# Token tiles and the first two weight units loaded and used in halves, constants and memory tokens loaded later

## The chip, the cores and the metric

The kernel runs on one core of one Trainium2 chip. Times are microseconds (us) of device time of one execution. The engines are TensorE (PE: matmuls and transposes, with PEld its weight loads), VectorE (DVE), ScalarE (ACT), GpSimd (POOL) and SyncE (SP), which issues nearly all transfers.

## What is computed

One inference step of a decoder layer, for a prompt of 256 tokens and 8 sample tokens together, so 264 columns of activations, with D_MODEL = 1024 and D_FF = 2816. Cut to its parts:

```python
x = x + 0.5 * swiglu_ffn(x, ffn1_norm, ffn1_w_in, ffn1_w_out)      # gate, up = split(rmsnorm(x) @ w_in); (silu(gate) * up) @ w_out
h = rmsnorm(x, mix_norm); proj = h @ w_in                          # pooling input, q, k, v, memory query
y = concat(pool_mixer, block-sparse attention over paged K/V, attention over 256 memory tokens)
x = x + y @ w_out
x = x + 0.5 * swiglu_ffn(x, ffn2_norm, ffn2_w_in, ffn2_w_out)
```

The memory keys and values of the prompt are computed here as well: `rmsnorm(mem_prompt) @ mem_w_kv`, and the keys are normed by head. The new keys, values and pooling state are outputs too.

## The kernel before

The kernel is one program written out by hand for each engine; semaphores order the engines, and each engine runs its own list in order. Activations lie transposed in SBUF: `xT` has 8 tiles of 128 channels by 264 tokens. Every matmul of a weight is done in three passes (`three`, L1381): a high part times a high part, high times low, low times high. So each weight unit of 128 x 1024 values goes through four steps: SP loads it into one of four `raw` buffers (`load_unit`, L414, issue on L421), ACT rounds it to `w_hi` (`split`, L632, L638), DVE subtracts to get `w_lo` (`split`, L910, L914), and PE runs 24 matmuls with it (L1383 to L1385), then raises `w_used`. The ring has RING = 4 slots: `load_unit` waits until DVE is through with the unit four before (`lo_ready`), and ACT's `split` waits until PE is through with it (`w_used`).

The first feed-forward has 44 such units, numbered 0 to 43 here; two of them (gate and up) give one of 22 hidden tiles. For each hidden tile DVE scales the gate (`gate`, L950), ACT does the Silu (L663), DVE scales the up half, multiplies, rounds and subtracts (`up_hidden`, L955 to L964). DVE's list for a pair of units is: split, gate, split, the four steps of up_hidden. ACT's list is: split, Silu, split. PE must wait for `gu_free`, raised by L955, before it writes over a pair of PSUM banks. Iterations 2 to 5 run in a loop on every engine, 6 to 10 stand singly because work on the memory tokens lies between them (`M_TURN_AT = 6`: PE transposes `m_rows` into four banks, ACT makes `m_hi` on L773, DVE `m_lo` on L1177). Four units of `mem_w_kv` follow, then 22 units of `ffn_w_out`.

The start, in program order. POOL sets constants. ACT loads `ident` and `gains` by its own queue. SP issues the sample tokens, the two prompt tiles (128 x 1024 each), units 0 to 3, `m_rows` (the memory tokens, 1 MB), the page table, nine constants, four pieces of `pool_w` and a copy of the pooling state; then it goes on with unit 4 and, from unit `EARLY_KEYS` = 7 on, pages of the key cache between the units. PE runs AWAKE = 20 matmuls on ones (each is two instructions in the profile, L1564), then 24 transposes of `x_rows` into 8 banks (L1391): the four lower tiles of sample and first prompt tile, then the four of the second prompt tile, then the upper four tiles. ACT copies the odd tiles out (L742) and rounds all eight to `x_hi` (L744, L746), two tiles per step of its loop, with `split(0)` and `split(1)` after the first two steps. DVE copies the even tiles (L1133), makes `x_lo` (L1138) and `w_lo`. PE then takes units 0 and 1 interleaved by channel tile. Behind that ACT squares the token rows (L754, with a root on L756, three times), DVE makes diagonals of the reciprocals and PE turns them into a row of scales (L1597). ACT goes on with split(4), split(5), the squares of the memory tokens (L762) and their root (L764), the load of the Silu table (L666), split(6).

## Time and profile before

| what | value |
|---|---|
| median of 3 runs | 602.05 us (600.65, 602.05, 602.41) |
| profiled execution, whole | 600.45 us |
| its span in the profile | 598.7 us |
| mean granted clock of PE | 0.991 |
| PE busy | 571.6 us, 95% of the span |
| DVE busy | 395.1 us, 66% |
| ACT busy | 263.5 us, 44% |
| DMA | 128.41 MB, mean 214 GB/s |

The profiled execution has 1.75 us around its span. It is 1.60 us below the median of the runs shown. A row of the timeline gives the start, the duration, the engine, the line, what is written and read, and in brackets the idle time before it with what ended it. Consecutive instructions of a line are merged into one row with their count.

### The profile page before, as it was taken

The page shows a single profiled execution, that of the slowest core. Times are in us where ns is not written, and L with a number is a line of the kernel's source. Part 1 is how long each engine was busy: PE and PEld are TensorE (multiplying, and loading weights), DVE is VectorE, ACT ScalarE, POOL GpSimd, SP SyncE. Part 2 cuts the span into 40 slices and gives each one's busy share as a digit, 9 for nine tenths or more (in the row PEclk, how much of TensorE's full clock was granted, in tenths as well). Part 3 has the DMA queues.
Part 4 walks back from the last instruction along what each step waited for, and adds up shares of the span by engine and source line. Part 5 has one row for each costly group of instructions (what it writes and reads, how often), then busy time and mean ns, then how long its engine had stood idle before and what let it go on. Part 6 is the DMA issues. An engine that isn't in the chain of part 4 may idle for free.

```text
span 598.7 us, 13514 instructions
## 1 busy us (share of the span) xinstructions
PE 571.6 (95%) x5124; PEld 524.9 (88%) x5124; DVE 395.1 (66%) x713; ACT 263.5 (44%) x410; POOL 16.1 (3%) x24
## 2 busy tenths in 40 slices
PE   7999999999999999999899758999999999999997
PEld 6999999999899997666567536989999999999996
DVE  3577677777598878699766530468767676774443
ACT  4843434534543337254376531474343434353331
POOL 1000000000000003000000000030000000000000
PEclk9899999999999999999999998999999999999999
DMA  9968778775677544997974799347665566575522
GB/s 284 293 177 249 224 227 239 223 235 177 211 233 276 193 142 139 327 386 219 372 261 140 237 358 362 96 117 211 175 176 174 171 178 174 180 236 185 175 71 73
DMA packets 132801, 128.41 MB, mean 214 GB/s; under 512 B 6560, under 2 KB 103927, under 8 KB 132751
## 3 DMA queue, kind: packets, MB, share of 16 engines
q1 hardware_dynamic: 132471, 127.76, 66.7%
q8 instruction: 26, 0.43, 0.3%
q10 hardware_dynamic: 288, 0.08, 0.1%
q14 instruction: 16, 0.13, 0.1%
HBM read 125.12 MB, written 2.83 MB: 214 GB/s over the span
## 4 chain that ended last, share of the span: by engine, by line
PE 69%; DVE 14%; issue 5%; ACT 4%; SPq 4%; DMA 3%; DVEq 0%; ACTq 0%; POOL 0%; POOLq 0%
PE banks L1383 21%; PE banks L1384 20%; PE banks L1385 20%; DVE w_lo L914 4%; DVE kv L925 3%; SPq L456 3%; ACT w_hi L638 2%; DMA kv<-in_cache_v 2%; PE banks L1522 2%; PE banks L1391 1%; SPq L442 1%; PE banks L1564 1%; PE banks L1798 1%; DMA raw<-in_ffn_w_in 1%; PE banks L1492 1%
## 5 line engine op out<-in xcount | busy, mean ns | idle before, releaser
L914 DVE TENSOR_TENSOR w_lo<-raw,w_hi 128x1024 fp32r<-128x1024 f32 x160 | 195.7, 1230 | 109.4 <-ACT w_hi L638 108.9
L1383 PE MATMUL banks<-x_hi,w_hi 128*128 128x264 f32 x768 | 222.1, 289 | 5.8 <-DVE w_lo L914 3.0
L1384 PE MATMUL banks<-x_lo,w_hi 128*128 128x264 f32 x768 | 218.4, 284 | 0.0
L1385 PE MATMUL banks<-x_hi,w_lo 128*128 128x264 f32 x768 | 218.2, 284 | 0.0
L638 ACT ACTIVATE w_hi<-raw 128x1024 fp32r<-128x1024 f32 x160 | 164.1, 1052 | 81.7 <-PE banks L1385 66.2
L1383 PEld LDWEIGHTS banks<-x_hi,w_hi 128*128 128x128 f32 x768 | 145.3, 189 | 10.4 <-issue 4.2
L1384 PEld LDWEIGHTS banks<-x_lo,w_hi 128*128 128x128 f32 x768 | 145.5, 189 | 0.0
L1385 PEld LDWEIGHTS banks<-x_hi,w_lo 128*128 128x128 f32 x768 | 144.8, 189 | 0.0
L1383 PE MATMUL banks<-h_hi,w_hi 128*128 (+1 forms) x352 | 100.3, 285 | 0.0
L1385 PE MATMUL banks<-h_hi,w_lo 128*128 (+1 forms) x352 | 100.2, 285 | 0.0
L1384 PE MATMUL banks<-h_lo,w_hi 128*128 (+1 forms) x352 | 100.0, 284 | 0.0
L663 ACT ACTIVATE sg<-sg 128x264 f32<-128x264 f32 x44 | 18.7, 426 | 142.1 <-DVE sg L950 142.1
L1384 PEld LDWEIGHTS banks<-h_lo,w_hi 128*128 128x128 f32 x352 | 66.5, 189 | 0.0
L1383 PEld LDWEIGHTS banks<-h_hi,w_hi 128*128 128x128 f32 x352 | 66.2, 188 | 0.3 <-ACT mem_kv L784 0.3
L1385 PEld LDWEIGHTS banks<-h_hi,w_lo 128*128 128x128 f32 x352 | 66.3, 188 | 0.0
L925 DVE STREAM_TRANSPOSE kv<-kv 128x1024 f32<-128x1024 f32 x32 | 38.6, 1228 | 0.0
L1383 PE MATMUL banks<-w_hi,x_hi 128*128 128x512 f32 x64 | 27.9, 435 | 0.8 <-DVE w_lo L914 0.7
L1385 PE MATMUL banks<-w_hi,x_lo 128*128 128x512 f32 x64 | 25.3, 395 | 0.0
L1384 PE MATMUL banks<-w_lo,x_hi 128*128 128x512 f32 x64 | 25.3, 395 | 0.0
L964 DVE TENSOR_TENSOR h_lo<-h_tmp,h_hi 128x264 f32 (+1 forms) x44 | 19.1, 434 | 3.6
L960 DVE TENSOR_TENSOR h_tmp<-sg,h_tmp 128x264 f32<-128x264 f32 x44 | 19.1, 433 | 2.6 <-ACT sg L663 1.3
L1798 PEld LDWEIGHTS banks<-kv,p_cols 128*8 128x8 f32 x512 | 13.4, 90 | 7.2 <-issue 7.2
(269 smaller groups left out, 498.2 us busy)
## 6 DMA issues: line engine op xcount, KB each, us to landing
raw<-in_ffn_w_in SPq DMA_DIRECT2D x88, 512.0 KB, 4.5
raw<-in_ffn_w_out SPq DMA_DIRECT2D x44, 512.0 KB, 3.4
kv<-in_cache_k SPq DMA_DIRECT2D x64, 256.0 KB, 5.1
kv<-in_cache_v SPq DMA_DIRECT2D x64, 256.0 KB, 4.8
raw<-in_w_in SPq DMA_DIRECT2D x12, 512.0 KB, 3.8
raw<-in_w_out SPq DMA_DIRECT2D x8, 512.0 KB, 6.0
raw<-in_mem_w_kv SPq DMA_DIRECT2D x4, 512.0 KB, 3.5
raw<-in_w_in SPq DMA_DIRECT2D x8, 256.0 KB, 3.7
```

Source lines behind the costliest of these rows:

```text
L456: sp.dma_start(kv[t % 4::4, slot, t // 4 * 2048:(t // 4 + 1) * 2048].rearrange("k (b c) -> k b c", b=4), cache[0, ds(page, 1)].rearrange(" ...
L638: act.activation(w_hi[:, n % RING, :], raw[:, n % RING, :], ACT.Copy).then_inc(hi_ready, 1)
L663: act.activation(sg[:, s, :], sg[:, s, :], ACT.Silu).then_inc(silu_ready, 1)
L914: vec.tensor_tensor(w_lo[:, n % RING, :], raw[:, n % RING, :], w_hi[:, n % RING, :].bitcast(F32), ALU.subtract).then_inc(lo_ready, 1)
L925: vec.transpose(key_pair(g), key_pair(g)).then_inc(k_turned8, 1)
L960: vec.tensor_tensor(h_tmp[:, s, :], sg[:, s, :], h_tmp[:, s, :], ALU.mult).then_inc(hm_ready, 1)
L964: vec.tensor_tensor(h_lo[:, ds(c, 1), :].rearrange("p a n -> p (a n)"), h_tmp[:, s, :], h_hi[:, ds(c, 1), :].rearrange("p a n -> p (a n)") ...
L1383: pe.matmul(out, lhs[0], rhs[0], start=start, stop=False)
L1384: pe.matmul(out, lhs[0], rhs[1], start=False, stop=False)
L1385: return pe.matmul(out, lhs[1], rhs[0], start=False, stop=stop)
L1522: mm = pe.matmul(bank[LG_BANK][32 * hp:32 * hp + 32, half * NP:(half + 1) * NP], q_cols[:, c0:c0 + 32], keys[:, 4 * hp + c], start=(b4 == ...
L1798: mm = pe.matmul(out, p_cols[:, 2 * half + t // 4, r0:r0 + 8], kv[:, slot, c0:c0 + P], start=False, stop=(b4 == 3 and t == PAGES - 1))
```

## The change

AWAKE goes from 20 to 10 and EARLY_KEYS from 7 to 8. The prompt tiles are loaded as four transfers of 128 x 512 instead of two of 128 x 1024; units 0 and 1 are loaded as two transfers of 4 x 128 columns each. ACT, DVE and PE use them by halves: PE transposes tiles 0 to 3 completely and then 4 to 7, ACT rounds half a unit after each of its four steps, DVE subtracts half a unit at a time, and PE runs unit 0 and then unit 1 over channel tiles 0 to 3, then both over 4 to 7. The page table, the constants, `m_rows`, `pool_w` and `band` are issued by SP at the ends of iterations 1 to 5 of the first feed-forward. ACT's squares of the memory tokens stand at the ends of iterations 4 and 5, their root behind the last Silu, with the Sqrt table loaded there instead of behind `mem_kv`; DVE's reciprocal of that root stands after the feed-forward.

```diff
--- before.py
+++ after.py
@@ -55,7 +55,7 @@
 TURN_BANKS = {5: 6, 0: 6, 1: 0, 2: 6, 3: 1, 4: 7}
 HY_BANKS, POOL_BANKS, MK_BANKS, QM_BANK = (6, 7, 4), (4, 5), (6, 4), 7
 ACT_PAGES = (0, 2, 4, 6)
-EARLY_PAIRS, AWAKE = 16, 20
+EARLY_PAIRS, AWAKE = 16, 10
 UNITS = 12
 X_BANKS = (4, 5, 6, 7, 0, 1, 2, 3)
 M_FIRST = (2, 3, 0, 1, 4, 5, 6, 7)
@@ -64,7 +64,7 @@
 J_ORDER = (2, 3, 0, 1)
 M_EARLY = (5, 6, 7, 0, 1, 3, 4)
 SQ_AFTER = (1, 3, 5)
-EARLY_KEYS, LATE_KEYS = 7, 9
+EARLY_KEYS, LATE_KEYS = 8, 9
 KV_SLOTS = 4
 KEPT = ("k", 0), ("k", 1), ("k", 6), ("k", 7)
 HELD = (4, 5, 6, 7)
@@ -247,6 +247,7 @@
         pg_loaded, poolw_loaded = sem("pg_loaded"), sem("poolw_loaded")
         raw_loaded = [sem(f"raw_loaded{i}") for i in range(RING)]
         kv_loaded = [[sem(f"kv_loaded{i}_{h}") for h in range(2)] for i in range(KV_SLOTS)]
+        first_loaded, first_hi, first_lo = [sem("first_loaded0"), sem("first_loaded1")], sem("first_hi"), sem("first_lo")
         hi_ready, lo_ready, w_used = sem("hi_ready"), sem("lo_ready"), sem("w_used")
         const_set = sem("const_set")
         lead_ready = sem("lead_ready")
@@ -477,25 +478,42 @@
                     sp.dma_start(kv[:, slot, :].rearrange("p (b t c) -> p b t c", b=NS, t=2),
                                  cache[0].rearrange("b (t p) h d -> p b t (h d)", p=P)).then_inc(kv_loaded[slot][0], 16)
 
+            def load_first(j, half):
+                col = j % 2 * DFF
+                sp.dma_start(raw[:, j, half * 512:(half + 1) * 512].rearrange("p (k c) -> p k c", k=4),
+                             ffn_in[0][:, 4 * half:4 * half + 4, col:col + P]).then_inc(raw_loaded[j] if half else first_loaded[j], 16)
+
             sp.dma_start(x_rows[0:NS, 0, :], a["x_sample"][:, 0, :]).then_inc(x_loaded[0], 16)
-            for t in range(2):
-                sp.dma_start(x_rows[:, 1 + t, :], a["x_prompt"][0, t * P:(t + 1) * P, :]).then_inc(x_loaded[t], 16)
-            for j in range(4):
+            for half in range(2):
+                for t in range(2):
+                    cols = slice(half * 512, half * 512 + 512)
+                    sp.dma_start(x_rows[:, 1 + t, cols], a["x_prompt"][0, t * P:(t + 1) * P, cols]).then_inc(x_loaded[half], 16)
+                load_first(half, 0)
+            for j in range(2):
+                load_first(j, 1)
+            for j in range(2, 4):
                 load_unit(U_FFN1, j, 0, ffn_in[0][:, :, (j // 2) * P + (j % 2) * DFF:(j // 2) * P + (j % 2) * DFF + P])
-            sp.dma_start(m_rows[:], a["mem_prompt"][0].rearrange("(t p) d -> p t d", p=P)).then_inc(m_loaded, 16)
-            sp.dma_start(page_ids[:], a["page_table"].rearrange("b g -> (b g)").unsqueeze(0)).then_inc(pg_loaded, 16)
-            for j, name in enumerate(("k_norm", "mem_k_norm", "q_norm")):
-                sp.dma_start(head_gain[:, j, :], a[name][0].partition_broadcast(P)).then_inc(c_loaded, 16)
-            for dst, name in ((rope, "rope"), (samp, "samp"), (rank, "rank"),
-                              (causal, "causal"), (band, "band")):
-                sp.dma_start(dst[:], a[name]).then_inc(c_loaded, 16)
-            sp.dma_start(ext[NS:P, :], a["state_pool"][0].rearrange("b j c -> (b j) c")).then_inc(c_loaded, 16)
-            sp.wait_ge(const_set, 2)
-            for g in range(4):
-                lo = HD * (g % 2)
-                sp.dma_start(pool_wd[lo:lo + HD, g // 2, lo:lo + HD], a["pool_w"][0, g]).then_inc(poolw_loaded, 16)
-            sp.dma_start(a["state_out"][0, :, 0:BUF - 1, :], a["state_pool"][0, :, 1:BUF, :]).then_inc(stored, 16)
-            sp.wait_ge(pg_loaded, 16)
+            def load_constants(i):
+
+                if i == 1:
+                    sp.dma_start(page_ids[:], a["page_table"].rearrange("b g -> (b g)").unsqueeze(0)).then_inc(pg_loaded, 16)
+                    for j, name in enumerate(("k_norm", "mem_k_norm", "q_norm")):
+                        sp.dma_start(head_gain[:, j, :], a[name][0].partition_broadcast(P)).then_inc(c_loaded, 16)
+                    sp.wait_ge(pg_loaded, 16)
+                elif i == 2:
+                    for dst, name in ((rope, "rope"), (samp, "samp"), (rank, "rank"), (causal, "causal")):
+                        sp.dma_start(dst[:], a[name]).then_inc(c_loaded, 16)
+                    sp.dma_start(ext[NS:P, :], a["state_pool"][0].rearrange("b j c -> (b j) c")).then_inc(c_loaded, 16)
+                elif i == 3:
+                    sp.dma_start(m_rows[:], a["mem_prompt"][0].rearrange("(t p) d -> p t d", p=P)).then_inc(m_loaded, 16)
+                elif i == 4:
+                    sp.wait_ge(const_set, 2)
+                    for g in range(4):
+                        lo = HD * (g % 2)
+                        sp.dma_start(pool_wd[lo:lo + HD, g // 2, lo:lo + HD], a["pool_w"][0, g]).then_inc(poolw_loaded, 16)
+                    sp.dma_start(a["state_out"][0, :, 0:BUF - 1, :], a["state_pool"][0, :, 1:BUF, :]).then_inc(stored, 16)
+                elif i == 5:
+                    sp.dma_start(band[:], a["band"]).then_inc(c_loaded, 16)
 
             pages_at = {EARLY_KEYS + p * 3 // 2: p for p in range(3 * PAGES)}
             for i in range(1, HT // 2):
@@ -504,6 +522,7 @@
                     load_unit(U_FFN1, j, i, ffn_in[0][:, :, col:col + P])
                     if 4 * i + j in pages_at:
                         load_page(*divmod(pages_at[4 * i + j], PAGES))
+                load_constants(i)
             for j in range(4):
                 load_unit(U_MEM, j, 0, w_mem[:, 2 * j:2 * j + 2, :])
             for k in range(HT):
@@ -744,8 +763,10 @@
                 act.activation(x_hi[:, odd - 1, :], xT[:, odd - 1, :], ACT.Copy, scale=gains[:, odd - 1:odd]).then_inc(xhi_ready, 1)
                 act.wait_ge(xT_act, pair + 1)
                 act.activation(x_hi[:, odd, :], xT[:, odd, :], ACT.Copy, scale=gains[:, odd:odd + 1]).then_inc(xhi_ready, 1)
-                if pair < 2:
-                    split(pair)
+                n, half = pair % 2, pair // 2
+                cols = slice(half * 512, half * 512 + 512)
+                act.wait_ge(raw_loaded[n] if half else first_loaded[n], 16)
+                act.activation(w_hi[:, n, cols], raw[:, n, cols], ACT.Copy).then_inc(hi_ready if half else first_hi, 1)
             split(2)
             split(3)
             junk = tmp[:].rearrange("p k n -> p (k n)")[:, 0:D]
@@ -757,22 +778,24 @@
                     .then_inc(xroot_ready, 1)
             split(4)
             split(5)
-            act.wait_ge(m_loaded, 16)
-            for t in range(2):
-                act.activation(m_junk[:, t, :], m_rows[:, t, :], ACT.Square, accum_out=ms[:, t:t + 1]).then_inc(ms_ready, 1)
-            act.wait_ge(ms_ready, 2)
-            act.activation(m_root[:], ms[:], ACT.Sqrt, bias=eps_col[:, 0:1], scale=1.0 / D).then_inc(mroot_ready, 1)
             table(ACT.Silu, 0)
             split(6)
             silu(0, 0, 0)
             ffn_second(0)
-            ffn_in_loop(0, 2, M_TURN_AT)
+            ffn_in_loop(0, 2, M_TURN_AT - 1)
+            act.wait_ge(m_loaded, 16)
+            act.activation(m_junk[:, 0, :], m_rows[:, 0, :], ACT.Square, accum_out=ms[:, 0:1]).then_inc(ms_ready, 1)
+            ffn_in_loop(0, M_TURN_AT - 1, M_TURN_AT)
+            act.activation(m_junk[:, 1, :], m_rows[:, 1, :], ACT.Square, accum_out=ms[:, 1:2]).then_inc(ms_ready, 1)
+            act.wait_ge(ms_ready, 2)
             for part in range(4):
                 for k in (2 * part, 2 * part + 1):
                     act.wait_ge(m_turned, k // 2 + 1)
                     act.activation(m_hi[:, k, :], bank[k // 2][:, (k % 2) * NP:(k % 2 + 1) * NP], ACT.Copy,
                                    scale=gains[:, 16 + k:17 + k]).then_inc(mhi_ready, 1)
                 ffn_in_loop(0, M_TURN_AT + part, M_TURN_AT + part + 1 if part < 3 else HT // 2)
+            table(ACT.Sqrt, 1)
+            act.activation(m_root[:], ms[:], ACT.Sqrt, bias=eps_col[:, 0:1], scale=1.0 / D).then_inc(mroot_ready, 1)
             for j in range(2, 6):
                 split(U_MEM + j)
             act.wait_ge(mrstd_ready, 1)
@@ -782,7 +805,6 @@
                 else:
                     act.wait_ge(w_used, U_MEM + 4)
                 act.activation(mem_kv[:, t, :], bank[t][:, :], ACT.Copy, scale=m_rstd[:, t:t + 1]).then_inc(mkv_ready, 1)
-            table(ACT.Sqrt, 1)
             ffn_out_loop(0, 0, 1)
             act.wait_ge(mkv_ready, 2)
             head_squares(0, ALL, mem_kv[:, :, 0:256])
@@ -1138,16 +1160,24 @@
                     vec.scalar_tensor_tensor(out=x_lo[:, m, :], in0=xT[:, m, :], scalar=gains[:, m:m + 1],
                                              in1=x_hi[:, m, :].bitcast(F32), op0=ALU.mult, op1=ALU.subtract).then_inc(xlo_ready, 1)
 
+            def split_half(n, half):
+                cols = slice(half * 512, half * 512 + 512)
+                vec.wait_ge(hi_ready if half else first_hi, n + 1)
+                vec.tensor_tensor(w_lo[:, n, cols], raw[:, n, cols], w_hi[:, n, cols].bitcast(F32), ALU.subtract)\
+                    .then_inc(lo_ready if half else first_lo, 1)
+
             x_copy(0)
             x_copy(2)
             x_lo_pair(0)
-            split(0)
+            split_half(0, 0)
+            x_lo_pair(1)
+            split_half(1, 0)
             x_copy(4)
-            x_lo_pair(1)
-            split(1)
             x_copy(6)
             x_lo_pair(2)
+            split_half(0, 1)
             x_lo_pair(3)
+            split_half(1, 1)
             split(2)
             split(3)
             vec.wait_ge(id_loaded, 16)
@@ -1166,8 +1196,6 @@
             gate(0, 0, 0, U_FFN1)
             up_hidden(0, 0, 0, U_FFN1)
             ffn_second(0)
-            vec.wait_ge(mroot_ready, 1)
-            vec.reciprocal(m_rstd[:], m_root[:]).then_inc(mrstd_ready, 1)
             ffn_in_loop(0, 2, M_TURN_AT)
             vec.wait_ge(ms_ready, 2)
             for part in range(4):
@@ -1178,6 +1206,8 @@
                                              scalar=gains[:, 16 + k:17 + k], in1=m_hi[:, k, :].bitcast(F32),
                                              op0=ALU.mult, op1=ALU.subtract).then_inc(mlo_ready, 1)
                 ffn_in_loop(0, M_TURN_AT + part, M_TURN_AT + part + 1 if part < 3 else HT // 2)
+            vec.wait_ge(mroot_ready, 1)
+            vec.reciprocal(m_rstd[:], m_root[:]).then_inc(mrstd_ready, 1)
             for j in range(2, 6):
                 split(U_MEM + j)
             vec.wait_ge(c_loaded, 16 * 9)
@@ -1563,28 +1593,24 @@
             for _ in range(AWAKE):
                 pe.matmul(bank[X_BANKS[KT - 1]][:, 0:P], ones[:], ones[:], start=True, stop=True)
             pe.wait_ge(id_loaded, 16)
-            pe.wait_ge(x_loaded[0], 32)
-            for m in range(4):
-                turn(bank[X_BANKS[m]][:, 0:NS], x_rows[0:NS, 0, m * P:(m + 1) * P], NS)
-                turn(bank[X_BANKS[m]][:, NS:NS + P], x_rows[:, 1, m * P:(m + 1) * P])
-            pe.wait_ge(x_loaded[1], 16)
-            for m in range(4):
-                turn(bank[X_BANKS[m]][:, NS + P:N], x_rows[:, 2, m * P:(m + 1) * P]).then_inc(x_turned, 1)
-            for m in range(4, KT):
+            pe.wait_ge(x_loaded[0], 48)
+            for m in range(KT):
+                if m == 4:
+                    pe.wait_ge(x_loaded[1], 32)
                 turn(bank[X_BANKS[m]][:, 0:NS], x_rows[0:NS, 0, m * P:(m + 1) * P], NS)
                 turn(bank[X_BANKS[m]][:, NS:NS + P], x_rows[:, 1, m * P:(m + 1) * P])
                 turn(bank[X_BANKS[m]][:, NS + P:N], x_rows[:, 2, m * P:(m + 1) * P]).then_inc(x_turned, 1)
             pe.wait_ge(const_set, 5)
             pe.wait_ge(xT_vec, 1)
             pe.wait_ge(xT_act, 1)
-            for k in range(KT):
-                pe.wait_ge(xlo_ready, k + 1)
+            for half in range(2):
                 for j in range(2):
-                    if k == 0:
-                        pe.wait_ge(lo_ready, j + 1)
-                    mm = three(bank[GU_BANK + j][:, 0:N], weights(j, k * P, (k + 1) * P), (x_hi[:, k, :], x_lo[:, k, :]),
-                               k == 0, k == KT - 1)
-                    if k == KT - 1:
+                    pe.wait_ge(lo_ready if half else first_lo, j + 1)
+                    for k in range(4 * half, 4 * half + 4):
+                        pe.wait_ge(xlo_ready, k + 1)
+                        mm = three(bank[GU_BANK + j][:, 0:N], weights(j, k * P, (k + 1) * P), (x_hi[:, k, :], x_lo[:, k, :]),
+                                   k == 0, k == KT - 1)
+                    if half:
                         mm.then_inc(w_used, 1)
             for j in range(2, 4):
                 pe.wait_ge((xT_vec, xT_act)[j % 2], 2)
```

## Rows read from the trace of the kernel before

**Rows 1.** Timeline of the first 17 us: PE, ACT and SP's queue.
```profile
1.00 3.35 PE L1564 MATMUL banks<-ones 128*128 128x128 f32 x14 [1.00 <-POOL ones L603]
...
7.60 4.25 PE L1391 MATMUL banks<-ident,x_rows 8*128 8x8 f32 x24
...
9.64 0.39 ACT L742 ACTIVATE xT<-banks 128x264 f32<-128x264 f32 x1 [6.39 <-PE banks L1391]
...
14.14 2.49 SPq L496 DMA_DIRECT2D pool_wd<-in_pool_w  x4
```

**Rows 2.** DMA issues at 1.64, 2.11 and 17.55 us: size, issue to landing.
```profile
x_rows<-in_x_prompt SPq DMA_DIRECT2D x1, 512.0 KB, 4.5
...
raw<-in_ffn_w_in SPq DMA_DIRECT2D x1, 512.0 KB, 5.9
...
raw<-in_ffn_w_in SPq DMA_DIRECT2D x1, 512.0 KB, 5.3
```

**Rows 3.** Timeline of ACT, one step of the start and splits 2, 3.
```profile
11.78 0.37 ACT L742 ACTIVATE xT<-banks 128x264 f32<-128x264 f32 x1
...
12.05 0.50 ACT L744 ACTIVATE x_hi<-xT,gains 128x264 fp32r<-128x264 f32 x1
...
12.87 1.05 ACT L638 ACTIVATE w_hi<-raw 128x1024 fp32r<-128x1024 f32 x1
...
16.62 2.00 ACT L638 ACTIVATE w_hi<-raw 128x1024 fp32r<-128x1024 f32 x2
```

**Rows 4.** Timeline of ACT from 22.9 to 29.6 us, splits 4, 5 and 6.
```profile
22.90 1.06 ACT L638 ACTIVATE w_hi<-raw 128x1024 fp32r<-128x1024 f32 x1 [0.18 <-DMA raw<-in_ffn_w_in]
24.68 1.06 ACT L638 ACTIVATE w_hi<-raw 128x1024 fp32r<-128x1024 f32 x1 [0.72 <-DMA raw<-in_ffn_w_in]
25.65 1.04 ACT L762 ACTIVATE m_junk<-m_rows 128x1024 f32<-128x1024 f32 x1
...
28.17 1.28 ACT L666 ACT_TABLE_LOAD   x1
...
29.57 1.04 ACT L638 ACTIVATE w_hi<-raw 128x1024 fp32r<-128x1024 f32 x1
```

**Rows 5.** Timeline of PE: first matmuls of units 2, 4, 8; around unit 16.
```profile
22.56 0.28 PE L1383 MATMUL banks<-x_hi,w_hi 128*128 128x264 f32 x1
...
29.26 0.37 PE L1383 MATMUL banks<-x_hi,w_hi 128*128 128x264 f32 x1
...
40.94 0.28 PE L1383 MATMUL banks<-x_hi,w_hi 128*128 128x264 f32 x1
...
64.11 0.28 PE L1385 MATMUL banks<-x_hi,w_lo 128*128 128x264 f32 x1
64.48 0.38 PE L1383 MATMUL banks<-x_hi,w_hi 128*128 128x264 f32 x1
```

**Rows 6.** Timeline of DVE in the first feed-forward: w_lo of units 8, 16, 20.
```profile
39.08 1.23 DVE L914 TENSOR_TENSOR w_lo<-raw,w_hi 128x1024 fp32r<-128x1024 f32 x1 [1.44 <-ACT w_hi L638]
...
62.78 1.23 DVE L914 TENSOR_TENSOR w_lo<-raw,w_hi 128x1024 fp32r<-128x1024 f32 x1 [1.44 <-ACT w_hi L638]
63.93 0.43 DVE L955 TENSOR_TENSOR h_tmp<-banks,rstd 128x264 f32<-128x264 f32 x1
...
74.86 1.23 DVE L914 TENSOR_TENSOR w_lo<-raw,w_hi 128x1024 fp32r<-128x1024 f32 x1 [1.45 <-ACT w_hi L638]
```

**Rows 7.** Waits from 30 to 150 us: total, times, longest.
```profile
ACT sg L663 <- DVE sg L950: 70.4, 22, 3.8
```

**Rows 8.** Windows: busy time (instructions) of PE, PEld, DVE, ACT, POOL; PEclk, DMA share, GB/s.
```profile
15.33:18.75 3.42, 3.28 (x15) 3.28 (x16) 3.10 (x7) 2.95 (x5) 0.00 (x0) 0.50 0.94 289
```

**Rows 9.** Timeline at the end of the first feed-forward, ACT, DVE and PE.
```profile
150.23 2.00 ACT L638 ACTIVATE w_hi<-raw 128x1024 fp32r<-128x1024 f32 x2
...
152.77 3.49 DVE L914 TENSOR_TENSOR w_lo<-raw,w_hi 128x1024 fp32r<-128x1024 f32 x3
...
155.39 0.39 PE L1383 MATMUL banks<-w_hi,m_hi 128*128 128x512 f32 x1
```

## The prediction, made before the changed kernel ran

> **What bounds the kernel now.** The page says that PE is busy nearly all the time, so I looked for the place where PE's pace comes from, in three steps. First the timeline of the start. PE runs its warm-up matmuls without a pause until the first transpose at 7.60, ACT gets its first tile at 9.64 [rows 1], and then ACT works without a gap until split(3); unit 2 starts on PE at 22.56 [rows 5]. Second, the transfers: the second prompt tile, issued at 1.64, lands 4.5 later, at 6.1, and unit 0, issued at 2.11, lands at 8.0 [rows 1, 2]. The queue passes 512 KB in about 1.9, so units 1, 2, 3 land at 9.9, 11.7, 13.6 (estimate), and behind them stand 1 MB of memory tokens and the constants: unit 4, issued at 17.55 [rows 2], lands at 22.9, where ACT waits for it [rows 4].
>
> Third, the first feed-forward. PE needs 40.94 - 29.26 = 11.68 for four units when nothing holds it [rows 5]. The same four units on DVE, from w_lo of unit 16 to that of unit 20, take 74.86 - 62.78 = 12.08 [rows 6]. ACT waits for DVE before each Silu, 22 times, 70.4 in all [rows 7], and DVE then waits 1.44 for ACT's w_hi [rows 6]: the two pass a baton round, split, up_hidden, split, gate, Silu, split. Neither waits for PE there, since a gate needs a unit that PE finished some 5 us before. And PE stops: after 64.11 it starts the next unit at 64.48, right behind the h_tmp of 63.93 that frees the banks [rows 5, 6]. So from about unit 15 to the end of that feed-forward PE follows the DVE and ACT round. **Its start decides**, the split of unit 6 at 29.57 [rows 4], and not PE's own start alone.
>
> **The change, part by part.**
> *Warm-up.* Twenty matmuls are 40 instructions, 14 of them take 3.35 [rows 1]. Half of them, 20, last from 1.0 to about 5.3 (a step is 0.21 at first, 3.35 less the long first one, over 14). The first halves of the prompt tiles have together as many bytes as one tile now; one tile lands 1.9 before 6.1, so 4.2, and with smaller packets up to 5.0. PE starts to transpose at 5.3 and not at 7.6: 2.2 earlier, with no pause between.
> *Transposes.* 24 take 4.25, three per tile, 0.53 [rows 1]. Tile 0 is ready at 5.9, tile 1 at 6.5, tile 3 at 7.5. The second halves lie behind 256 KB of unit 0: 6.1 + 0.95 + 0.1 = 7.2, in time. Tiles 4 to 7 are ready at 8.0 to 9.6. ACT can start at 6.6 and not at 9.64, because its tile no longer waits for four transposes of the other prompt tile.
> *ACT's four steps.* A copy is 0.27 from start to start, two roundings 0.82, a unit 0.95 [rows 3]. Half a unit I put at 0.58, between a half (0.48) and a whole (0.95), near the half since a rounding of 264 columns is 0.41. A step is 1.67, four are 6.7. One stall comes in: DVE has its copy of tile 4 behind the half splits of units 0 and 1. Half a w_lo I put at 0.6 (half of 1.23), so DVE reaches the copy at 10.8, is done at 11.2 (0.43, as its other operations on 264 columns, [rows 6]), and ACT has waited 0.9. Split(2) starts at 6.6 + 6.7 + 0.9 = 14.3, now 16.62 [rows 3]: 2.3 earlier. By bounds of 0.48 and 0.95 for the half it is 2.7 or 0.8.
> *PE.* It takes unit 0 lower half at 9.6 (behind its last transpose), unit 1 lower at 11.1, unit 0 upper at 13.5, unit 1 upper at 15.2 (w_lo ends then), each 12 matmuls of 0.121 = 1.5. Unit 2 starts at 16.6, when its w_lo is there, and not at 22.56: 5.9 earlier.
> *Units 4 and 5.* Unit 4 is issued when w_lo of unit 0 is whole, at 13.5, with an empty queue: even with the 5.3 of today [rows 2] it lands at 18.8. ACT wants it 2.3 earlier than 22.90 - 0.18, at 20.4. That wait goes, and of the 24.68 of unit 5 another 0.84 (0.72 of it shown as idle). Together 1.0.
> *Squares and root of the memory tokens.* Between split(5), 24.68, and the table load, 28.17, lie 3.49; without them 1.06: 2.4 less [rows 4]. Split(6) comes 2.3 + 1.0 + 2.4 = 5.8 earlier, at 23.8.
> *Where they go.* One square (1.04 [rows 4], and some 0.2 of readout) comes in between the even and the odd split of ACT, at the ends of iterations 4 and 5. DVE takes the odd one only after w_lo (1.15, from 62.78 to 63.93 [rows 6]) and the four steps of up_hidden (some 0.4 each), 2.75 after the even w_hi; ACT has it ready at 0.95. With 1.23 it is 2.2: hidden, with 0.6 to spare. At the second place the m_hi copies come on top, but DVE's m_lo too. Bounds: 0, or 1.2 each.
> *Moved loads.* 14.14 to 16.63 for four `pool_w` [rows 1]: 0.62 each. By this row a small issue costs up to 0.6, so with eleven others and the larger `m_rows` it is about 9 of SP time (estimate), in five pieces of up to some 3. Behind each stands the load of a unit. Such a load is issued when w_lo of the unit four before is there: for unit 20 at 64.0, and its split is at 73.8 (its w_lo begins at 74.86, less 1.05) [rows 6]. That is 9.8, for an odd unit less, about 7.5 (estimate); the load takes up to 5.3 [rows 2], so 2 to 4 are spare. The dearest piece is `m_rows`, 1 MB, 3.8 of the queue before unit 16, which has about 9.8 as unit 20. I take 0, up to 3 in all. Pages one unit later: nothing, they are used in the second matmul stage. SP's wait for the page table holds unit 8 until some 23 to 24, when its own condition (w_lo of unit 4, 22.7) comes as well, and its split is due at 32.
> *Sqrt table.* 1.28 and 0.3 of root are now before the splits of the third and fourth memory unit, at 150.23 [rows 9]. The first of them is then 1.8 late, but DVE took it only at 152.77 [rows 9], so its w_lo comes 0.4 later, at 154.4 in today's times, and PE wants it at 155.39 [rows 9]. Nothing, and DVE's m_rstd hides too. The table behind `mem_kv` goes, beside PE's work: nothing. Without this cover it would be 0.4.
>
> **Sum.** The round of DVE and ACT starts 5.8 earlier, PE is 5.9 earlier at unit 2, and would arrive at unit 8 with today's margin. Everything after is ordered by PE and by buffers that PE frees, the page loads of the attention as well, so the shift goes through to the end. 600.45 - 5.8 = 594.65 for the profiled execution; the median is 1.60 above it, so 596.25 on that base. Between the two, nearer the median, I take **595.9**.
>
> **The clock.** Today PE has two gaps at 13.6 and before, and 15.33 to 18.75 runs at half the granted clock, 0.50, that is 1.2 GHz and not 2.4 [rows 8]. In the changed kernel the gaps are shorter (12.5 to 13.5, a few tenths at 15). If it falls again for one such stretch, PE loses 3.42 x 0.5 = 1.7. But PE loses some 0.4 per four units to the round anyway, so this is covered later: nothing, or at most 0.5 by the row of scales (L1597) for split(6). The Trainium skill ("TensorE: Matmul & The Clock Gate", Part 1: The HAM clock gate) says that the throttled state is the default and that activity releases it, which speaks against halving the warm-up. By that rule the transposes could run at the low clock; the rows agree that gaps cost the clock.
>
> **Rivals.**
> (A) Part of it stays (0.22). ACT's chain is shortened less: half units cost near whole ones (2.7 - 0.8, so 1.5 lost), or both squares show in the round (2.4 lost), or unit 5 is late. Gain 2 to 4.3, around 3.4: 598.7. For: the margin of 0.6 is thin. Against: DVE's order puts 2.75 there.
> (B) Transposes at the half clock (0.08). A matmul at half clock is 0.22 and not 0.12, so four tiles cost 1.7 more, ACT's tile 1 comes 0.5 later and tile 5 about 1.2: gain 4.6, 597.4.
> (C) It does not show (0.06). PE starts earlier, but the attention stage or the page loads are tied to something that does not move, and the gain is waited away: 602. Against: its loads wait for buffers that PE frees.
> (D) Slower (0.06). SP's issues become part of the round: each piece of constants in the feed-forward holds a unit's load beyond its split, and PE stands. Place: units 8 to 24. If all 9 count, it is 602.05 - 5.8 + 9 = 605.3. It decides when more than 2 to 4 per piece is held. Against: ACT waits for a load only twice today, 0.9 in all, both before unit 6.
> (E) Halves cost the queue a fixed part each (0.02). Tile to unit lands 1.9 apart for 512 KB although one transfer takes 4.5 to land: 2.6 is fixed and hidden now. If it fell on each of the four added transfers, unit 3 would land 10.4 later, at 24.0, 8.8 after its split is due: 602.05 - 5.8 + 8.8 = 605.0. The Trainium skill ("DMA: Bandwidth & Descriptors", Rules for kernel authors) advises 1 MiB or more per transfer and to merge small ones, so by it the halves lose; the rows, with transfers that follow each other closely, speak against a loss of this size.
> The forecast itself has 0.56.
>
> **Numbers.** The forecast's own range is 594.0 to 597.3. With (A) and (B) I go to 593.6 and 599.6; above lie (C), (D) and (E), 0.14. A measurement of this kernel can tell about 0.3%, 1.8 us, from no change. Faster by more: forecast, (B) and most of (A), 0.85. Within: 0.08. Slower: 0.07.
>
> **What the profile would show.** First transpose at 5.3 with no gap before; ACT's first tile at 6.6; split(2) at 14.3 with an idle piece of 0.9 before the rounding of tile 4; unit 2 on PE at 16.6; no ACT wait for DMA on units 4 and 5; split(6) at 23.8; w_lo of unit 20 at 69.1; no DVE wait for w_hi above 1.5 at units 23 and 27; the first matmul of the third memory unit at 149.6. The prediction is wrong if ACT waits for `raw` in the feed-forward, if the four-unit step of DVE grows beyond 12.1, or if gaps later on PE grow by what was won.

## The result, and the profile after

The changed kernel takes **594.88 us** (median; 593.37 to 598.02), the kernel before, beside it, 602.23: ratio 0.9888 [0.984, 0.9936], 1.1% faster. A second set of runs of the same kernel, the first experiment below, gave 595.44 against 601.77, ratio 0.9892 [0.9866, 0.9919]. The forecast was 595.9, within 593.6 to 599.6.

The profiled execution of the first set, 598.02 us, is the longest of its set. Its page, in the order busy time, share, instructions; then groups with busy time, mean, idle time before and what ended most of it:

```profile
PE 570.7 (96%) x5104; PEld 523.9 (88%) x5104; DVE 395.5 (66%) x715; ACT 263.1 (44%) x412; POOL 16.1 (3%) x24
...
L936 DVE TENSOR_TENSOR w_lo<-raw,w_hi 128x1024 fp32r<-128x1024 f32 x158 | 193.2, 1230 | 106.6 <-ACT w_hi L657 105.6
```

The page looks like the one before: nearly all that changed lies in the first 30 us. The timeline of that execution answers to [rows 1], [rows 3], [rows 5] and [rows 4]:

```profile
1.00 4.64 PE L1594 MATMUL banks<-ones 128*128 128x128 f32 x20 [1.00 <-POOL ones L622]
...
6.29 6.60 PE L1421 MATMUL banks<-ident,x_rows 8*128 8x8 f32 x24 [0.66 <-DMA x_rows<-in_x_prompt]
...
15.45 1.99 ACT L657 ACTIVATE w_hi<-raw 128x1024 fp32r<-128x1024 f32 x2
...
16.87 0.42 PE L1414 MATMUL banks<-x_lo,w_hi 128*128 128x264 f32 x1
17.09 0.35 PE L1415 MATMUL banks<-x_hi,w_lo 128*128 128x264 f32 x1
17.27 0.29 PE L1413 MATMUL banks<-x_hi,w_hi 128*128 128x264 f32 x1
17.39 0.28 PE L1414 MATMUL banks<-x_lo,w_hi 128*128 128x264 f32 x1
...
24.86 1.04 ACT L657 ACTIVATE w_hi<-raw 128x1024 fp32r<-128x1024 f32 x1
...
27.51 0.43 DVE L1193 COPY rstd<-banks 128x264 f32<-128x264 f32 x1 [2.62 <-PE banks L1623]
...
27.86 1.22 DVE L936 TENSOR_TENSOR w_lo<-raw,w_hi 128x1024 fp32r<-128x1024 f32 x1
```

Two things are to be seen. PE runs at half speed until about 17.1: the 24 transposes take 6.60 where [rows 1] has 4.25, and a matmul step, from one start to the next, is 0.22 up to there and 0.12 from there. And split(6), at 24.86, is not what holds w_lo of unit 6: DVE could have w_hi at 25.90, but stands 2.62 for PE's row of scales (L1623), copies it to `rstd` at 27.51, and starts w_lo(6) only then, at 27.86. w_lo(6) reads nothing of that row. It waits for it because the copy stands ahead of it in DVE's list, and DVE runs its list in order. Below, w_lo(6) is the number to follow. In the kernel before, its two neighbours on DVE were:

```profile
29.54 0.43 DVE L1163 COPY rstd<-banks 128x264 f32<-128x264 f32 x1 [2.53 <-PE banks L1597]
...
30.65 1.23 DVE L914 TENSOR_TENSOR w_lo<-raw,w_hi 128x1024 fp32r<-128x1024 f32 x1 [0.68 <-ACT w_hi L638]
```

There the copy, PE's side, ends at 29.97 (29.54 + 0.43), and ACT's w_hi(6) at 30.61 [rows 4]: **two engines nearly tied**, 0.6 apart.

### The profile page after: what moved, and what is told of

The parts are those of the page before. It is cut to its first block, busy times and chain, and to the rows that moved or that the text cites. A ratio compares the mean times of both kernels' runs of the same rounds, so it can differ in the third digit from the quotient of the medians.

```text
span 596.2 us, 13483 instructions
## 1 busy us (share of the span) xinstructions
PE 570.7 (96%) x5104; PEld 523.9 (88%) x5104; DVE 395.5 (66%) x715; ACT 263.1 (44%) x412; POOL 16.1 (3%) x24
## 4 chain that ended last, share of the span: by engine, by line
PE 75%; DVE 8%; SPq 5%; DMA 4%; issue 4%; ACT 4%; DVEq 0%; ACTq 0%
PE banks L1413 22%; PE banks L1414 22%; PE banks L1415 22%; PE banks L1421 3%; PE banks L1552 2%; DVE w_lo L936 2%; ACT w_hi L657 2%; SPq L457 2%; DMA kv<-in_cache_mem_k 2%; DMA kv<-in_cache_v 1%; SPq L443 1%; DVE kv L947 1%; PE banks L1824 1%; DMA x_rows<-in_x_prompt 1%; PE banks L1522 1%
## 5 line engine op out<-in xcount | busy, mean ns | idle before, releaser
L936 DVE TENSOR_TENSOR w_lo<-raw,w_hi 128x1024 fp32r<-128x1024 f32 x158 | 193.2, 1230 | 106.6 <-ACT w_hi L657 105.6
L657 ACT ACTIVATE w_hi<-raw 128x1024 fp32r<-128x1024 f32 x158 | 161.7, 1050 | 80.2 <-PE banks L1415 71.9
L1824 PE MATMUL banks<-kv,p_cols 128*8 128x128 f32 x512 | 15.9, 280 | 5.2 <-DMA kv<-in_cache_v 5.2
```

Of the source, the lines that this page charges most:

```text
L657: act.activation(w_hi[:, n % RING, :], raw[:, n % RING, :], ACT.Copy).then_inc(hi_ready, 1)
L936: vec.tensor_tensor(w_lo[:, n % RING, :], raw[:, n % RING, :], w_hi[:, n % RING, :].bitcast(F32), ALU.subtract).then_inc(lo_ready, 1)
L1824: mm = pe.matmul(out, p_cols[:, 2 * half + t // 4, r0:r0 + 8], kv[:, slot, c0:c0 + P], start=False, stop=(b4 == 3 and t == PAGES - 1))
```

## The experiments

The theory, R in the texts on record, is the prediction's: the round of DVE and ACT paces the first feed-forward, and its start decides. The text for after_again, written with the first profile at hand, already lets it start at the later of split(6) and the row of scales; the numbers forecast for moved_only still follow split(6) alone. The main rival, P: PE is busy all the time, and its own start decides. Each ran beside the kernel before, which had medians of 601.77, 601.75 and 601.58 in the three sets. Times from the profiles, in us: PE's first matmul of unit 2, ACT's split(6), DVE's w_lo(6), the last matmul of unit 43 (where the first feed-forward's gates end on PE), and the way from w_lo(6) to it.

| kernel | median | unit 2 | split(6) | w_lo(6) | unit 43 | way |
|---|---|---|---|---|---|---|
| before | 601.8 | 22.56 | 29.57 | 30.65 | 149.82 | 119.2 |
| after, first profile | 594.88 | 20.55 | 24.86 | 27.86 | 147.49 | 119.6 |
| after_again | 595.44 | 18.25 | 23.92 | 25.56 | 145.22 | 119.7 |
| awake20 | 595.77 | 18.57 | 25.52 | 26.60 | 146.26 | 119.7 |
| halves_only | 601.76 | 18.94 | 30.63 | 31.70 | 150.66 | 119.0 |
| moved_only | 601.09 | 23.63 | 26.96 | 30.96 | 149.97 | 119.0 |
| scales_early | 595.11 | 19.76 | 24.03 | 25.11 | 144.76 | 119.7 |
| moved_scales | 597.85 | 23.11 | 26.53 | 27.61 | 147.50 | 119.9 |
| pe_delay | 595.47 | 16.88 | 23.83 | 24.91 | 144.56 | 119.7 |
| act_delay | 597.57 | 18.86 | 26.42 | 27.50 | 147.33 | 119.8 |
| x_halves | 599.59 | 22.04 | 25.37 | 29.35 | 148.35 | 119.0 |
| squares_front | 597.38 | 18.93 | 26.42 | 27.50 | 147.13 | 119.6 |
| before_awake10 | 600.35 | 20.74 | 30.69 | 31.77 | 150.82 | 119.1 |
| scales_awake12 | 595.12 | 17.74 | 24.71 | 25.78 | 145.41 | 119.6 |

The median less w_lo(6) is 569.2 to 570.6 in eleven of the fourteen rows, while w_lo(6) itself moves by 6.8: the time follows w_lo(6) nearly one for one. The others are before (571.2), before_awake10 (568.6), and the first profile of after (567.0), which is of the longest execution of its set.

**after_again** is the changed kernel, unedited.

> The changed kernel, untouched, for a second profile. Theory R (the round of DVE and ACT in the first feed-forward sets its end; the round starts at the later of ACT's split(6) and the row of scales, which PE makes behind unit 3): the ratio to before stays near 0.988, and where the granted clock is full during the transposes, unit 2 starts on PE at 16.6 and split(6) at 23.8, w_lo of unit 20 begins at 69.1 and the execution takes 594 to 595. Where the clock is 0.5 until 17 as in the first profile, 598. Rival K (the spread between executions has nothing to do with the clock at the start): the second profile shows the same start whatever its time.

Measured: 595.44, ratio 0.9892 [0.9866, 0.9919]; the profiled execution took 594.74, against 598.02 in the first set, with this start:

```profile
1.00 3.96 PE L1594 MATMUL banks<-ones 128*128 128x128 f32 x20 [1.00 <-POOL ones L622]
5.93 2.13 PE L1421 MATMUL banks<-ident,x_rows 8*128 8x8 f32 x12 [0.98 <-DMA x_rows<-in_x_prompt]
...
7.12 0.39 ACT L761 ACTIVATE xT<-banks 128x264 f32<-128x264 f32 x1 [3.87 <-PE banks L1421]
...
8.89 2.17 PE L1421 MATMUL banks<-ident,x_rows 8*128 8x8 f32 x12 [0.82 <-DMA x_rows<-in_x_prompt]
...
11.55 0.52 ACT L763 ACTIVATE x_hi<-xT,gains 128x264 fp32r<-128x264 f32 x1 [0.82 <-DVE xT L1155]
...
14.51 1.99 ACT L657 ACTIVATE w_hi<-raw 128x1024 fp32r<-128x1024 f32 x2
...
22.52 1.28 ACT L685 ACT_TABLE_LOAD   x1
...
23.92 1.04 ACT L657 ACTIVATE w_hi<-raw 128x1024 fp32r<-128x1024 f32 x1
...
25.21 0.43 DVE L1193 COPY rstd<-banks 128x264 f32<-128x264 f32 x1 [1.26 <-PE banks L1623]
...
25.56 1.22 DVE L936 TENSOR_TENSOR w_lo<-raw,w_hi 128x1024 fp32r<-128x1024 f32 x1
```

The transposes ran at full speed here; the clock was low only for a stretch of PE's first units (windows: busy time and instructions of PE, PEld, DVE, ACT, POOL; PEclk, DMA share, GB/s):

```profile
10.00:14.00 4.00, 4.00 (x22) 3.79 (x22) 3.70 (x9) 3.18 (x9) 0.00 (x0) 0.61 0.96 238
```

It is the same kernel twice, and rival K, the same start in both, is out. With the low clock until 17.1, w_lo(6) is 2.3 later (27.86 for 25.56), and the execution 3.3 longer; the other 1.0 lies behind unit 43, where nothing ties it to the clock of the start. ACT has only 0.94 of the 2.3 (split(6) at 24.86 for 23.92), and by ACT alone w_lo(6) would have been at 25.90. The rest is PE's row of scales.

**awake20** puts the warm-up back to its old length.

```diff
-EARLY_PAIRS, AWAKE = 16, 10
+EARLY_PAIRS, AWAKE = 16, 20
```

> The changed kernel with 20 warm-up matmuls again. Theory R: the transposes cannot start before 7.5, or 9.6 where the clock stays low, ACT is 2.2 later throughout, so half of the gain of the front goes: about 2.2 slower than the changed kernel, some 597.5, ratio 0.992. Rival W (the warm-up buys the clock, and a short one costs more than it frees): as fast as the changed kernel or faster, 593 to 595, ratio 0.988 or below.

Measured: 595.77, ratio 0.9899 [0.9873, 0.9924], 0.3 from after_again. A loss of 2.2 was expected; the medians show none, but the interval just reaches the 0.992 of R. The profile shows half of it:

```profile
26.60 1.23 DVE L936 TENSOR_TENSOR w_lo<-raw,w_hi 128x1024 fp32r<-128x1024 f32 x1 [0.57 <-ACT w_hi L657]
```

On PE the late start of the transposes, 7.52, is paid back by the clock: they run whole and at full speed, 4.25 for 24, and PE reaches unit 2 at 18.57, where after_again, with a stretch at the low clock, is at 18.25. ACT isn't paid back: split(6) is 1.60 later, and w_lo(6) 1.04. Whether the longer warm-up loses that 1.0 these runs can't tell.

**halves_only** keeps the halves and the short warm-up, but has the constants, the memory tokens, the squares and the root where the kernel before has them.

```diff
-            def load_constants(i):
...
+            sp.dma_start(m_rows[:], ...)      # and all constants, ahead of ffn_in_loop
...
+            for t in range(2):
+                act.activation(m_junk[:, t, :], m_rows[:, t, :], ACT.Square, ...)
```

> Halves and the short warm-up, but constants, memory tokens, their squares and root where they were. Theory R: unit 4 lands at 22.9 as before and the squares stand before split(6), so split(6) stays at 29.6 and the time at that of before within 1 us, ratio 1.000. Rival P (PE's own start sets the end): unit 2 starts at 16.6, unit 4 waits for its w_lo until 25.2, and 4 us are won, ratio 0.993.

Measured: 601.76, ratio 1.0001 [0.9984, 1.0018]. **The halves alone bring nothing**, though PE starts unit 2 3.6 earlier:

```profile
23.84 1.06 ACT L649 ACTIVATE w_hi<-raw 128x1024 fp32r<-128x1024 f32 x1 [2.73 <-DMA raw<-in_ffn_w_in]
...
27.98 0.42 DVE L1184 COPY rstd<-banks 128x264 f32<-128x264 f32 x1
...
30.63 1.04 ACT L649 ACTIVATE w_hi<-raw 128x1024 fp32r<-128x1024 f32 x1
31.70 1.23 DVE L927 TENSOR_TENSOR w_lo<-raw,w_hi 128x1024 fp32r<-128x1024 f32 x1 [3.30 <-ACT w_hi L649]
```

ACT waits 2.73 for unit 4, which stands behind the memory tokens in the queue, and its split(6) is at 30.63. PE's side was done at 28.40. R had forecast this result, and P, with 4 us won, is out.

**moved_only** has the constants, squares and root moved, but the tiles and units 0 and 1 whole and the long warm-up.

```diff
-                load_first(half, 0)
+                sp.dma_start(x_rows[:, 1 + t, :], a["x_prompt"][0, t * P:(t + 1) * P, :])...
...
-EARLY_PAIRS, AWAKE = 16, 10
+EARLY_PAIRS, AWAKE = 16, 20
```

> Constants, memory tokens, their squares and root moved, but tiles and units whole and 20 warm-up matmuls. Theory R: split(2) stays at 16.6, the waits for units 4 and 5 (1.0) and the squares (2.4) go, split(6) at 26.1, 3.4 us won, ratio 0.994. Rival P: unit 2 stays at 22.56 on PE and nothing is won, ratio 1.000. Rival D (the loads between the units hold the ring): slower than before.

Measured: 601.09, ratio 0.9982 [0.9965, 0.9999]: a gain of 0.7 where 3.4 was expected. Split(6) did come 2.6 earlier, at 26.96, but:

```profile
26.96 1.04 ACT L646 ACTIVATE w_hi<-raw 128x1024 fp32r<-128x1024 f32 x1
29.54 1.03 PE L1606 MATMUL banks<-x_diag,ones 8*128 8x8 f32 x6
30.61 0.43 DVE L1172 COPY rstd<-banks 128x264 f32<-128x264 f32 x1 [3.62 <-PE banks L1606]
30.96 1.22 DVE L923 TENSOR_TENSOR w_lo<-raw,w_hi 128x1024 fp32r<-128x1024 f32 x1
```

DVE has w_hi(6) at 28.00, but the row of scales, which PE makes behind unit 3 at 29.54, only at 30.61 (the 3.62 of the line count from the end of w_lo(5)). PE was at unit 2 1.07 later than in the profile of before, and the stretch from 14 to 18 us has a granted clock of 0.50 here and 0.67 there, so part of this lateness may be the chance of one execution. Here the sum that follows split(6) alone fell. The theory from here on: w_lo(6) starts at the later of two, w_hi(6) of ACT and the row of scales of PE (R2 in the texts on record). The test is to move one side alone.

**scales_early** is the changed kernel with the row of scales between units 2 and 3.

```diff
+                if j == 2:
+                    for t in range(3):
...
+                    mm.then_inc(xr_psum, 1)
```

> The changed kernel with PE's row of scales between units 2 and 3 instead of behind unit 3. Theory R2 (the round of DVE and ACT starts at w_lo of unit 6, which waits for two things, ACT's split(6) and the row of scales): w_lo of unit 6 begins right behind split(6), 25.0 in place of 25.6 where the clock was up early, 25.9 in place of 27.9 in an execution like the first profile of the changed kernel; 0.5 to 2 us won over the changed kernel, 594, ratio 0.987. Rival P (PE's own start sets the end): no change, or 0.5 slower where PE waits for the diagonals.

Measured: 595.11, ratio 0.988 [0.9848, 0.9912]. The copy moves to 23.97 and w_lo(6) stands right behind ACT:

```profile
23.97 0.42 DVE L1193 COPY rstd<-banks 128x264 f32<-128x264 f32 x1
...
25.11 1.23 DVE L936 TENSOR_TENSOR w_lo<-raw,w_hi 128x1024 fp32r<-128x1024 f32 x1 [0.71 <-ACT w_hi L657]
```

That is 0.45 earlier than in after_again, and nothing that the medians can tell.

**moved_scales** is moved_only with the same edit.

> moved_only (constants, memory tokens and their squares moved; tiles and units whole, 20 warm-up matmuls) with the row of scales between units 2 and 3. Theory R2: moved_only won only 0.7 because its split(6) ended at 28.0 but the row of scales came at 30.9 behind unit 3; now w_lo of unit 6 begins at 28.1, 2.5 before the kernel before, and about 2.5 us are won, ratio 0.996. Rival P: PE's units stand where they stood, so as moved_only, ratio 0.998.

Measured: 597.85, ratio 0.9946 [0.9922, 0.997].

```profile
27.18 0.43 DVE L1172 COPY rstd<-banks 128x264 f32<-128x264 f32 x1 [0.63 <-PE banks L1607]
27.61 1.23 DVE L923 TENSOR_TENSOR w_lo<-raw,w_hi 128x1024 fp32r<-128x1024 f32 x1
...
29.88 0.28 PE L1392 MATMUL banks<-x_hi,w_hi 128*128 128x264 f32 x1
...
147.50 0.28 PE L1394 MATMUL banks<-x_hi,w_lo 128*128 128x264 f32 x1
```

The same few matmuls that are worth 0.3 in the changed kernel, less than the medians can tell, are worth 3.2 here (601.09 to 597.85), and w_lo(6) came 3.35 earlier. This is the run that carries the theory: without any halves, and with PE later than before at unit 2 (23.11 for 22.56) and at unit 4 (29.88 for 29.26), 3.9 of the 6.3 are there, and unit 43 ends 2.3 earlier, because both sides of the wait came earlier.

It also shows where the theory ends. From unit 4 to unit 43 PE waits for nothing in this profile (busy 115.00 of the 115 us from 30 to 145, against 114.16 in after_again) and takes 117.62. That is the least that PE needs, and here PE itself sets the last matmul of unit 43: the way is 119.9, where moved_only has 119.0. Of the 0.9, 0.36 come at the first step, where ACT's split(7) waits 0.5 for PE to be through with unit 3.

**pe_delay** puts 20 matmuls, which nothing uses, on PE behind the row of scales and before unit 4.

```diff
+            for r in range(20):
+                pe.matmul(bank[GU_BANK_2][:, 0:N], x_hi[:, 0, 0:P], x_hi[:, r % KT, :], start=True, stop=True)
```

> The changed kernel with 20 more matmuls of 264 columns on PE between the row of scales and unit 4, 2.4 us of work that nothing uses. Theory R2: PE waits for the round some 2.6 us in all between unit 8 and unit 43, so nearly all of it is absorbed: within 0.6 us of the changed kernel, ratio 0.990. Rival P: 2.4 us slower, ratio 0.993.

Measured: 595.47, ratio 0.9903 [0.987, 0.9935].

```profile
22.84 1.02 PE L1623 MATMUL banks<-x_diag,ones 8*128 8x8 f32 x6
23.62 2.69 PE L1626 MATMUL banks<-x_hi 128*128 128x264 f32 x20
...
26.15 0.28 PE L1413 MATMUL banks<-x_hi,w_hi 128*128 128x264 f32 x1
```

Unit 4 starts 3.31 behind the row of scales (22.84) and not 0.79, as in after_again (24.14 to 24.93), and the time stays: PE catches up before unit 43, and the last matmul there is at 144.56, earlier than in after_again (the interval of the medians just holds P's 0.993, the profile doesn't). So the first feed-forward is not PE's stage, though PE is busy in it nearly all the time. But it isn't far from being so. From unit 4 to the last matmul of unit 43 PE had 120.3 in after_again, of the 117.6 that it needs (moved_scales): 2.7 to spare. Here it has 118.4, so 0.8 was left. With a warm-up of 10 it also is a profile with the clock at full from the start: unit 2 is at 16.88. By that, PE without the added work would have been at unit 4 some 1.3 before after_again; of the 2.4 added, 1.2 is a delay against that kernel, and w_lo(6) is no later for it.

**act_delay** puts two copies of 1056 columns, which nothing uses, on ACT ahead of the Silu table.

```diff
+            for r in range(2):
+                act.activation(tmp[:, 4 * r:4 * r + 4, :], xT[:, 4 * r:4 * r + 4, :], ACT.Copy)
```

> The changed kernel with two more copies of 1056 columns on ACT ahead of the Silu table, 2.1 us of work that nothing uses. Theory R2: split(6) comes 2.1 later, w_lo of unit 6 1.6 later (0.5 were a wait for the row of scales), and the end 1.6 later than the changed kernel, ratio 0.992. Rival P: ACT idles more than half of its time and PE has its units in store, so no change, ratio 0.989.

Measured: 597.57, ratio 0.992 [0.9891, 0.9948].

```profile
22.97 2.04 ACT L782 ACTIVATE tmp<-xT 128x1056 f32<-128x1056 f32 x2
...
26.42 1.05 ACT L657 ACTIVATE w_hi<-raw 128x1024 fp32r<-128x1024 f32 x1
27.50 1.23 DVE L938 TENSOR_TENSOR w_lo<-raw,w_hi 128x1024 fp32r<-128x1024 f32 x1 [1.25 <-ACT w_hi L657]
```

2.04 on ACT cost 2.1 at the median against after_again, where 1.6 was expected; 2.4 on PE cost nothing. Split(6) is 2.50 later in this profile, 0.57 of it from a slower start (split(2) at 15.08 for 14.51), and w_lo(6) 1.94, since in after_again it stood 0.6 behind w_hi(6), for PE.

**x_halves** is moved_only with the short warm-up and the token tiles alone in halves.

```diff
+            for half in range(2):
+                for t in range(2):
+                    sp.dma_start(x_rows[:, 1 + t, cols], a["x_prompt"][0, t * P:(t + 1) * P, cols])...
```

> The changed kernel with only the token tiles in halves: units 0 and 1 are loaded, split and used whole, PE takes them interleaved as before. Theory R2: ACT reaches split(2) at 14.3 as in the changed kernel and split(6) at 23.8, but PE has w_lo of unit 1 only at 13.1 and starts unit 2 at 20.3, so the row of scales comes at 27 and w_lo of unit 6 begins at 27.5, 2 later than in the changed kernel: 597.4, ratio 0.992. Rival H (the half units are worth nothing, ACT alone counts): as the changed kernel, ratio 0.989.

Measured: 599.59, ratio 0.9977 [0.9963, 0.9991], above what either reading gave: unit 2 was expected at 20.3 and came at 22.04, w_lo(6) at 27.5 and came at 29.35. In its profile PE has the low clock, 0.50, for ten microseconds, and DVE again waits for PE:

```profile
9.10:19.30 10.20, 8.20 (x34) 6.82 (x34) 8.20 (x14) 9.22 (x17) 0.00 (x0) 0.50 0.89 232
```

```profile
29.00 0.43 DVE L1174 COPY rstd<-banks 128x264 f32<-128x264 f32 x1 [3.61 <-PE banks L1604]
```

With units 0 and 1 whole, PE stands between them (8.20 busy of 10.20), and its earlier start is lost at 0.50 of the clock. So what the unit halves are worth, 4.2 between this kernel and the changed one, may be in part the clock, and this run can't part the two.

**squares_front** is the changed kernel with the memory tokens behind unit 3 in the queue and the squares and the root ahead of the Silu table again.

```diff
+            act.wait_ge(m_loaded, 16)
+            for t in range(2):
+                act.activation(m_junk[:, t, :], m_rows[:, t, :], ACT.Square, ...)
...
             table(ACT.Silu, 0)
```

> The changed kernel with the memory tokens loaded behind unit 3 and their squares and root ahead of the Silu table again; the constants stay among the units. Theory R2: split(6) 2.4 later than in the changed kernel, 26.4, w_lo of unit 6 at 27.5 against 25.6, the end 1.9 later: 597.4, ratio 0.992. Rival L (what counts is the waiting for loads of units 4 and 5, the squares hide in ACT's idle time): as the changed kernel, ratio 0.989.

Measured: 597.38, ratio 0.9936 [0.9916, 0.9955]: 1.9 more than after_again, with split(6) 2.5 and w_lo(6) 1.94 later. What the squares cost at the old place is what they save at the new one, and inside the round they cost nothing that shows.

**before_awake10** is the kernel before with the short warm-up.

```diff
-EARLY_PAIRS, AWAKE = 16, 20
+EARLY_PAIRS, AWAKE = 16, 10
```

> The kernel before with 10 warm-up matmuls and nothing else changed. Theory R2: the transposes start at about 6.3, but unit 4 still lands at 22.9 and split(6) stays at 29.6: no difference, ratio 1.000. Rival P: PE starts everything 1.3 earlier and 1.3 us are won, ratio 0.998; rival W (the clock is lost): slower than before by 1 to 2 us, ratio 1.002 to 1.003.

Measured: 600.35, ratio 0.9989 [0.9971, 1.0006]. The interval holds R2's 1.000 and P's 0.998 alike, and only W is out. The profile speaks against P: PE is 1.8 earlier at unit 2, ACT's split(6) is not earlier, and unit 43 ends at 150.82, 1.0 later than in the profile of before.

```profile
31.77 1.23 DVE L914 TENSOR_TENSOR w_lo<-raw,w_hi 128x1024 fp32r<-128x1024 f32 x1 [3.31 <-ACT w_hi L638]
```

**scales_awake12** is scales_early with a warm-up of 12.

> The changed kernel with the row of scales between units 2 and 3 and 12 warm-up matmuls, which fill the 0.7 that PE waits for the token tiles. Theory R2: w_lo of unit 6 begins at 25.1 whatever the clock does at the start, and PE, now the tighter of the two, loses less often: 594.5, ratio 0.987. Rival: no difference from the changed kernel that can be measured, ratio 0.989.

Measured: 595.12, ratio 0.9896 [0.9872, 0.9919], as scales_early. No version here is shown to beat the changed kernel.

## Why the prediction was right, point by point

**The size.** Forecast -5.8 on the profiled execution; measured 600.45 to 594.74, -5.7, where the transposes ran at the full clock, -2.4 in the first profile, and medians 6.3 apart in the larger sets. At w_lo(6) 5.1 of it is there, at the last matmul of unit 43 4.6. The rest is not placed: from there to the end the fourteen profiles differ by 2.5 among themselves (449.3 to 451.8), and the profiled execution of before lies 1.3 below its median. In the two kernels that keep its order of loads, halves_only and before_awake10, w_lo(6) is at 31.70 and 31.77, 1.1 later than in it, at medians that can't be told from its own; that its profile shows a start better than its usual one would fit, and is only argued.

**What sets the end: half right.** That the round of DVE and ACT paces the first feed-forward, and that its start decides, held: from w_lo(6) to the last matmul of unit 43 it is 119.0 to 119.9, wherever w_lo(6) lies between 24.91 and 31.77, and only in moved_scales does PE set the end of it. pe_delay and act_delay show which engines are in it. The step that failed is "Its start decides, the split of unit 6", with the row of scales priced at 0.5 at most. The start has two conditions, and I followed one. With a good clock the error was small: predicted w_lo(6) is 23.8 + 1.05 = 24.9, measured 25.56, of it 0.6 for the scales. That is luck in part, since nothing in the sum asked when PE's side would come; the halves happened to bring it along. The picture with one condition still gives the right answer for halves alone (0, as unit 4 and the squares hold split(6)), but for moved work alone it gives 3.4, and that brought 0.7. The terms don't add: 0 and 0.7 alone, 6.3 together. Halves alone leave ACT's side at 31.7, moving alone leaves PE's side at 31.0, and each by itself stays where before was. Not tried: w_lo(6) ahead of the copy in DVE's list, which would take it out of the wait for PE.

**Warm-up and tiles.** Predicted first transpose 5.3, measured 5.93, with 0.98 of wait for the tiles: the first halves were put at 4.2 to 5.0, an estimate, and no row gives their landing. The second halves were put at 7.2, "in time"; the last was issued at 3.12 and took 5.7, so it landed at 8.8, and PE stands 0.82 for it before the transposes at 8.89. ACT doesn't feel that, since it comes to those tiles later. ACT's first tile 7.12 for 6.6. The idle piece before the rounding of tile 4 is 0.82 for 0.9, split(2) 14.51 for 14.3 (the terms written down, 6.6 + 6.7 + 0.9, give 14.2). Half a unit on ACT is 0.52 from start to start, put at 0.58; half a w_lo on DVE 0.68, put at 0.6. The late first tile and the cheaper half units nearly cancel.

**Units 4, 5 and split(6).** No wait for `raw` is left on ACT, and split(6) is at 23.92 for 23.8: the term of 5.8 on ACT was right to 0.2 in this profile; in the first one it is 4.7 (24.86).

**PE at unit 2.** 18.25 for 16.6, and 20.55 in the first profile, both with stretches at the low clock. In pe_delay, where the clock held, it is 16.88.

**The clock.** Rival (B), transposes at the half clock, came true in the first profile, at 598.02 for its 597.4. The nearness of the two is luck: (B) made ACT 1.2 later, and ACT was 0.94 later, while most of the loss came by PE. The prediction's own step, "nothing, or at most 0.5", failed there, for the reason above: PE's side is a condition of w_lo(6), so w_lo(6) came 2.3 later than in after_again. A row shows that it isn't the rule: full speed for all 24 transposes in after_again (2.13 and 2.17 for 12). The Trainium skill ("TensorE: Matmul & The Clock Gate", Part 1: The HAM clock gate) says that how many matmuls run slow at the start of an execution varies from run to run of one kernel; the profiles agree: in one execution of this kernel the clock was low up to 17.1, through all the transposes, in the other only from about 10.9 to 14.3. That halving the warm-up would lose by it, a doubt that the prediction took from the same section, did not show: awake20, with the warm-up twice as long, is 0.3 from after_again and not faster.

**Squares, table, moved loads.** Hidden, as predicted. Between 30 and 145 us no wait of DVE for w_hi is longer than 1.4, and ACT's wait for DVE before Silu is 3.3 on the mean (65.9 in 20), as it was 3.2 (70.4 in 22, up to 150 us) [rows 7]. The rows are total, times, longest:

```profile
ACT sg L682 <- DVE sg L972: 65.9, 20, 4.0
DVE w_lo L936 <- ACT w_hi L657: 25.9, 18, 1.4
DVE w_lo L936 <- issue: 0.8, 4, 0.2
```

So (D) and (E) are out: ACT doesn't wait for a load in that stretch, nor for units 2 to 5, so the halved transfers don't cost a fixed part each. (A) is out by the half units (0.52) and by squares_front, whose way is 119.6 without squares in the round. (C) is out by the measured gain. What the prediction put at nothing is in the last row: four waits of DVE, 0.8 in all, in which it waits for nothing that the profile shows, ahead of w_lo of units 11, 15, 19 and 23, once in each turn of DVE's loop.

**w_lo(20)** was predicted at 69.1 and came at 70.20; the first matmul of the third memory unit at 149.6 and came at 150.79.

```profile
70.20 1.23 DVE L936 TENSOR_TENSOR w_lo<-raw,w_hi 128x1024 fp32r<-128x1024 f32 x1 [1.44 <-ACT w_hi L657]
...
150.79 0.39 PE L1413 MATMUL banks<-w_hi,m_hi 128*128 128x512 f32 x1
```

Of the 1.1, 0.65 is w_lo(6)'s. The rest, 0.4, lies in the round (44.64 from w_lo(6) to w_lo(20), for 44.21 before), as does the longer way to unit 43, 119.6 to 119.8 for 119.0 to 119.2. It goes with those four waits: the eight profiles of kernels with both halves and moved loads have them, 0.8 in each, and the other six profiles have at most one, of 0.11, whenever their w_lo(6) starts. (moved_scales has a way of 119.9 without them, but by PE, as said above.) The squares are not their cause, since squares_front has them without squares in the round. What it is stays open. The change costs some 0.5 by it.
